# Last layer norm of tile 1's front half built from turned moment rows and two-row products, its input weighted early on GpSimd

## What is computed

```python
def layer_norm(x, g, b):
    mu = jnp.mean(x, axis=-1, keepdims=True)
    var = jnp.mean(jnp.square(x - mu), axis=-1, keepdims=True)
    return (x - mu) * lax.rsqrt(var + LN_EPS) * g + b

hdn = jnp.square(jax.nn.relu(jnp.einsum('bsd,df->bsf', x, w_ff1[l])))
ff_out = jnp.einsum('bsf,fd->bsd', hdn, w_ff2[l])
x = layer_norm(DEEPNORM_ALPHA * x + ff_out, ln2_g[l], ln2_b[l])
```

## Time and profile before

| | |
|---|---|
| device time, median of 3 runs | 1088.48 us (1087.71 to 1088.55) |
| the profiled execution: its own time | 1088.89 us |
| the profiled execution: its span | 1087.1 us, granted TensorE clock 1.000 |
| busy, share of the span: PE, PEld | 1081.4 us (99%), 918.4 us (84%) |
| busy, share of the span: DVE, ACT, POOL | 822.6 us (76%), 578.2 us (53%), 24.5 us (2%) |
| transfers | 213.84 MB, mean 197 GB/s |

### The profile page before, as it was taken

One profiled execution on the slowest core, in us unless ns is written; L12 is line 12 of the kernel. 1 busy time (PEld: TensorE's weight loads), 2 busy tenths in 40 slices (PEclk: granted clock), 3 DMA queues, 4 the chain that ended last, 5 costly groups with the idle time before them and its releaser, 6 DMA issues.

```text
span 1087.1 us, 13951 instructions
## 1 busy us (share of the span) xinstructions
PE 1081.4 (99%) x5586; PEld 918.4 (84%) x5586; DVE 822.6 (76%) x923; ACT 578.2 (53%) x756; POOL 24.5 (2%) x43
## 2 busy tenths in 40 slices
PE   9999999999999999999999999999999999999998
PEld 7888888888888888888888888888888888888886
DVE  6587758666666685667699999766776678889998
ACT  6487757665544524445465456444454455545461
POOL 1000101010000000000000000000000000000000
PEclk9999999999999999999999999999999999999999
DMA  9857665557545835665656566566656655655862
GB/s 300 263 177 224 185 191 156 175 177 247 176 155 168 285 108 156 192 193 176 218 189 231 169 220 232 167 188 191 191 174 204 219 177 198 228 195 190 282 222 78
DMA packets 108048, 213.84 MB, mean 197 GB/s; under 512 B 6784, under 2 KB 38016, under 8 KB 107472
## 3 DMA queue, kind: packets, MB, share of 16 engines
q1 hardware_dynamic: 107216, 209.61, 60.1%
q0 software_dynamic: 624, 3.21, 1.0%
q10 hardware_dynamic: 144, 0.13, 0.0%
HBM read 210.83 MB, written 2.10 MB: 196 GB/s over the span
## 4 chain that ended last, share of the span: by engine, by line
PE 98%; DVE 1%; DMA 1%; issue 0%; SPq 0%; ACT 0%; DVEq 0%
PE low_ps L802 11%; PE low_ps L639 10%; PE high_ps L802 9%; PE high_ps L824 7%; PE high_ps L823 7%; PE high_ps L822 7%; PE low_ps L531 6%; PE low_ps L527 6%; PE low_ps L529 6%; PE low_ps L808 5%; PE high_ps L808 5%; PE low_ps L644 5%; PE low_ps L823 3%; PE low_ps L824 3%; PE low_ps L822 3%; PE high_ps L576 1%
## 5 line engine op out<-in xcount | busy, mean ns | idle before, releaser
L1333 DVE TENSOR_TENSOR w_lo<-w_raw,w_hi 128x1024 fp32r<-128x1024 f32 x175 | 213.1, 1222 | 133.6 <-ACT w_hi L993 132.2
L993 ACT ACTIVATE w_hi<-w_raw 128x1024 fp32r<-128x1024 f32 x175 | 185.1, 1059 | 188.5 <-PE low_ps L531 69.5
L802 PE MATMUL low_ps<-x1T,w_hi 128*128 128x512 f32 x512 | 177.3, 393 | 0.0
L802 PE MATMUL high_ps<-x1T,w_hi 128*128 128x512 f32 x448 | 155.1, 393 | 0.0
L639 PE MATMUL low_ps<-xT,w_hi 128*128 128x512 f32 x448 | 144.2, 398 | 0.0
L808 PE MATMUL low_ps<-x1T,w_lo 128*128 128x256 f32 x512 | 139.3, 278 | 0.0
L1663 DVE TENSOR_TENSOR w_lo<-w_raw,w_hi 128x1024 fp32r<-128x1024 f32 x72 | 87.0, 1222 | 59.7 <-ACT w_hi L1194 59.7
L1218 ACT ACTIVATE sum_hi<-sum_raw 128x1024 fp32r<-128x1024 f32 x60 | 63.6, 1063 | 124.7 <-DVE sum_raw L1685 112.8
L808 PE MATMUL high_ps<-x1T,w_lo 128*128 128x256 f32 x448 | 122.1, 278 | 0.0
L1194 ACT ACTIVATE w_hi<-w_raw 128x1024 fp32r<-128x1024 f32 x72 | 76.1, 1060 | 86.4 <-PE low_ps L802 43.4
L802 PEld LDWEIGHTS low_ps<-x1T,w_hi 128*128 128x128 f32 x512 | 94.9, 187 | 20.1
(11 more groups left out here) (214 smaller groups left out, 1915.4 us busy)
## 6 DMA issues: line engine op xcount, KB each, us to landing
w_raw<-in_w_ff SPq DMA_DIRECT2D x208, 512.0 KB, 4.3
w_raw<-in_w_in SPq DMA_DIRECT2D x93, 512.0 KB, 4.3
more_raw<-in_w_ff SPq DMA_DIRECT2D x42, 512.0 KB, 5.2
w_raw<-in_w_out SPq DMA_DIRECT2D x32, 512.0 KB, 3.7
x_raw<-in_x_turned SPq DMA_DIRECT2D x8, 256.0 KB, 6.4
y<-in_x SPq DMA_DIRECT2D x8, 256.0 KB, 4.6
side_raw<-in_w_ff SPq DMA_DIRECT2D x4, 512.0 KB, 6.7
w_raw<-in_w_in SPq DMA_DIRECT2D x6, 256.0 KB, 5.8
```

Source lines behind the costliest of these rows:

```text
L802: return pe.matmul(banks[:, b, :], w_hi[:, slot, cols], x1T[:, t, :, :].rearrange("p h t -> p (h t)"), start=(t == 0 and not lows_open), s ...
L993: act.activation(w_hi[:, slot, :], w_raw[:, slot, :], ACT.Copy).then_inc(w_rounded, units)
L1333: dve.tensor_tensor(w_lo[:, slot, :], w_raw[:, slot, :], w_hi[:, slot, :].bitcast(F32), ALU.subtract).then_inc(w_split, units)
```

## The change

Tile 1's front half (pieces 3 to 6) is no longer centred by VectorE. The norm is written as (y*g - mean*g + std*b) / std:

- GpSimd multiplies tile 1's front half by g in place, once g and b are loaded and the fourth of the front half's statistics is taken (`y2_stats` 4); then it raises the semaphore `weighted`. Its powers for 1/std stand behind that in its list.
- TensorE puts identity times the weighted y into PSUM for the four pieces. When tile 1's moments are there, it turns the two columns [mean, std] of `mean_std` into two rows by a product with the identity; ScalarE copies these with the signs -1 and +1 into `moment_rows`; TensorE adds the product of these two rows with the two rows [g, b] (`gb_rows`).
- ScalarE takes std with a square root (`last_std`), ahead of tile 1's epsilon instruction; a first square root on a constant stands ahead of the tail. ScalarE copies pieces 3 to 6 out with 1/std as the scale.
- SP loads the two rows of `gb_rows` (4 KB each) behind each broadcast load of g and b.
- Piece 2 is finished by VectorE, last, and stored last by SP; the products and the diagonal for it go. VectorE's order behind tile 1's moments is: centre 7, centre 8, finish 7, finish 8, finish piece 2.
- The stores' order becomes 0, 1, 3, 7, 4, 8, 5, 2 (6 still by ScalarE).
- At the start VectorE fills two more small vectors (`eps_one`, `row_signs`).

The diff without the declarations of tiles and semaphores and without the reshaped helper of the first norm (`first_scale` and `inverse_std`, which issue the same instructions for that norm as `norm_scale(0)` did):

```diff
-COPIED = [2] + SCALED
-STORE_ORDER = [0, 1, 2, 7, 3, 4, 5, 8]
+FIRST_HALF = slice(0, HALF)
+BY_VECTOR = [0, 1, 7, 8, 2]
+STORE_ORDER = [0, 1, 3, 7, 4, 8, 5, 2]
...
+                    sp.dma_start(gb_rows[n:n + 1, :], v[:, FIRST_HALF]).then_inc(rows_loaded, 16)
...
-            if i in COPIED:
-                sp.wait_ge(y2_copied, COPIED.index(i) + 1)
+            if i in SCALED:
+                sp.wait_ge(y2_copied, SCALED.index(i) + 1)
             else:
-                sp.wait_ge(y2_ready, i + 1 - len([n for n in COPIED if n < i]))
+                sp.wait_ge(y2_ready, BY_VECTOR.index(i) + 1)
...
-        pe.wait_ge(tail_summed, 2)
-        pe.wait_ge(gb2_loaded, 32)
-        pe.matmul(high_ps[:, 1, :], ident_t[:, :], ln2_gb[:, 1, LAST_PIECES[2][1]], start=True, stop=False)
-        pe.wait_ge(diag_ready, 1)
-        pe.wait_ge(centred, len(PIECES) + 3)
-        pe.matmul(high_ps[:, 1, :], diag[0][:, :], y1[:, 0, LAST_PIECES[2][1]], start=False,
-                  stop=True).then_inc(y2_scaled, 1)
         pe.wait_ge(low_drained, 4)
+        pe.wait_ge(weighted, 1)
         for i in SCALED:
-            pe.matmul(scaled_ps(i), ident_t[:, :], ln2_gb[:, 1, LAST_PIECES[i][1]], start=True,
-                      stop=False)
-        pe.wait_ge(diag_ready, TT)
-        for n, i in enumerate(SCALED):
-            tt, cols = LAST_PIECES[i]
-            pe.wait_ge(centred, len(PIECES) + (6 if i > 4 else 4))
-            pe.matmul(scaled_ps(i), diag[1][:, :], y1[:, tt, cols], start=False,
+            pe.matmul(scaled_ps(i), ident_t[:, :], y1[:, 1, LAST_PIECES[i][1]], start=True, stop=False)
+        pe.wait_ge(tail_summed, 3)
+        pe.wait_ge(moments, 2 * TT)
+        pe.wait_ge(mean_std_ready, 1)
+        pe.matmul(high_ps[0:2, 2, 0:P], mean_std, ident_t[:, :], start=True, stop=True).then_inc(
+            moments_turned, 1)
+        pe.wait_ge(rows_loaded, 32)
+        pe.wait_ge(rows_ready, 1)
+        for i in SCALED:
+            pe.matmul(scaled_ps(i), moment_rows[0:2, :], gb_rows[0:2, LAST_PIECES[i][1]], start=False,
                       stop=True).then_inc(y2_scaled, 1)
...
-        for tt in range(TT):
-            act.wait_ge(moments, TT + tt + 1)
-            act.activation(var_eps[:, tt:tt + 1], mean_var[:, 2 * tt + 1:2 * tt + 2], ACT.Copy,
-                           bias=EPS).then_inc(var_ready, 1)
-            if tt == 1:
-                act.wait_ge(y2_scaled, 1)
-                act.activation(y1[:, 0, LAST_PIECES[2][1]], high_ps[:, 1, :], ACT.Copy).then_inc(
-                    y2_copied, 1)
-            act.wait_ge(std_ready, TT + tt + 1)
-            act.activation(diag[tt][:, :], ident_t[:, :], ACT.Copy, scale=inv_std[:, tt:tt + 1]).then_inc(
-                diag_ready, 1)
+        act.wait_ge(powers_ready, 5)
+        act.activation(last_std, eps_one, ACT.Sqrt)
+        act.wait_ge(moments, TT + 1)
+        act.activation(var_eps[:, 0:1], mean_var[:, 1:2], ACT.Copy, bias=EPS).then_inc(var_ready, 1)
+        act.wait_ge(moments, TT + 2)
+        act.activation(last_std, mean_var[:, 3:4], ACT.Sqrt, bias=eps_one).then_inc(mean_std_ready, 1)
+        act.activation(var_eps[:, 1:2], mean_var[:, 3:4], ACT.Copy, bias=EPS).then_inc(var_ready, 1)
+        act.wait_ge(moments_turned, 1)
+        act.activation(moment_rows[0:2, :], high_ps[0:2, 2, 0:P], ACT.Copy, scale=row_signs[0:2, :]).then_inc(
+            rows_ready, 1)
+        act.wait_ge(std_ready, 2 * TT)
         for n, i in enumerate(SCALED):
             tt, cols = LAST_PIECES[i]
-            act.wait_ge(y2_scaled, n + 2)
-            act.activation(y1[:, tt, cols], low_ps[:, n, 0:cols.stop - cols.start],
-                           ACT.Copy).then_inc(y2_copied, 1)
+            act.wait_ge(y2_scaled, n + 1)
+            act.activation(y1[:, tt, cols], low_ps[:, n, 0:cols.stop - cols.start], ACT.Copy,
+                           scale=inv_std[:, 1:2]).then_inc(y2_copied, 1)
         for i in BY_SCALAR:
             tt, cols = LAST_PIECES[i]
-            act.wait_ge(y2_copied, SCALED.index(i) + 2)
+            act.wait_ge(y2_copied, SCALED.index(i) + 1)
             act.dma_start(out_d[:, tt, cols], y1[:, tt, cols]).then_inc(stored, 16)
...
+        dve.memset(eps_one, EPS).then_inc(powers_ready, 1)
+        dve.memset(row_signs, 1.0).then_inc(powers_ready, 1)
+        dve.wait_ge(powers_ready, 4)
+        dve.memset(row_signs[0:1, :], -1.0).then_inc(powers_ready, 1)
...
-        def finish_piece(i, centred_before):
-            finish_norm(1, count + centred_before, 1, LAST_PIECES[i][1], y1, ln2_gb, y2_ready)
-
-        centre(1, 1, slice(0, 512), y1, ln2_gb)
         centre(1, 1, LAST_PIECES[7][1], y1, ln2_gb)
-        finish_piece(7, 5)
-        centre(1, 1, slice(512, 1024), y1, ln2_gb)
         centre(1, 1, LAST_PIECES[8][1], y1, ln2_gb)
-        finish_piece(8, 7)
+        finish_norm(1, count + 4, 1, LAST_PIECES[7][1], y1, ln2_gb, y2_ready)
+        finish_norm(1, count + 5, 1, LAST_PIECES[8][1], y1, ln2_gb, y2_ready)
+        finish_norm(1, count + 3, 0, front[2], y1, ln2_gb, y2_ready)
...
+        pool.wait_ge(gb2_loaded, 32)
+        pool.wait_ge(y2_stats, 4)
+        pool.tensor_tensor(y1[:, 1, FIRST_HALF], y1[:, 1, FIRST_HALF], ln2_gb[:, 0, FIRST_HALF],
+                           ALU.mult).then_inc(weighted, 1)
+        inverse_std(1, 0)
+        inverse_std(1, 1)
```

More of the change, by code:

```diff
@@ L175, in hybrid_layer @@
     mid = at("mid", [P, 2 * TT, NC], F32, 48 * KB)
-    diag = [at(f"diag{tt}", [P, P], F32, 48 * KB + 512 * tt) for tt in range(TT)]
+    moment_rows = at("moment_rows", [P, P], F32, 48 * KB)
     X0 = 56 * KB
@@ L221, in hybrid_layer @@
     last_raw = at("last_raw", [P, 4 * NC], F32, H0 + 24 * KB)
+    gb_rows = at("gb_rows", [P, HALF], F32, X0 + 28 * KB)
     own_hi = [at("own_hi0", [P, 3 * NC], F32R, H0 + 77 * KB), at("own_hi1", [P, 3 * NC], F32R, X0)]
@@ L244, in hybrid_layer @@
     eps_sum = part(42, 2)
+    last_std, eps_one, row_signs = part(40, 1), part(44, 1), part(45, 1)
+    mean_std = small[:, 34:41:6]
     stats = part(48, TT * CHUNKS * 6 + 6)
@@ L313, in hybrid_layer @@
     y2_stats, y2_ready, stored = sem("y2_stats"), sem("y2_ready"), sem("stored")
-    diag_ready, y2_scaled, y2_copied = sem("diag_ready"), sem("y2_scaled"), sem("y2_copied")
+    rows_loaded, mean_std_ready, moments_turned = sem("rows_loaded"), sem("mean_std_ready"), sem("moments_turned")
+    rows_ready, y2_scaled, y2_copied = sem("rows_ready"), sem("y2_scaled"), sem("y2_copied")
+    weighted = sem("weighted")
     x_d = x.rearrange("b (t p) d -> p (b t) d", p=P)
@@ L1919, in rms_scale, with inverse_std, first_scale @@
             pool.tensor_tensor(o_scale, root, inv_sums[h % 3][:, 0:4:2], ALU.mult).then_inc(scale_ready, 1)
[L1921 to L1931, removed]
+        def inverse_std(norm, tt):
+            n = TT * norm + tt + 1
+            pool.wait_ge(var_ready, n)
+            pool.tensor_tensor(inv_std[:, tt:tt + 1], var_eps[:, tt:tt + 1],
+                               minus_half[:, tt:tt + 1], ALU.pow).then_inc(std_ready, 1)
+        def first_scale(tt):
+            pool.wait_ge(moments, tt + 1)
+            pool.tensor_scalar(var_eps[:, tt:tt + 1], mean_var[:, 2 * tt + 1:2 * tt + 2], EPS,
+                               None, ALU.add).then_inc(var_ready, 1)
+            inverse_std(0, tt)
         pool.wait_ge(w_used, SLOTS + 1)
@@ L1947, in gpsimd_program @@
                 "p l d -> p (l d)")).then_inc(gb1_loaded, 16)
-        norm_scale(0)
-        norm_scale(1)
+        for tt in range(TT):
+            first_scale(tt)
+        pool.wait_ge(gb2_loaded, 32)
[4 more added lines that the diff above has]
+        inverse_std(1, 1)
     with nc.Block() as block:
```

## The result

| | before | after |
|---|---|---|
| device time, median | 1088.31 us (1087.71 to 1089.05, 15 runs) | 1090.48 us (1089.60 to 1091.81, 15 runs) |
| ratio after / before, 95% interval | | 1.0020 (1.0013 to 1.0027) |
| the profiled execution: its own time, span | 1088.89, 1087.1 us | 1090.55, 1088.7 us |
| granted clock, mean of the span | 1.000 | 0.997 |

The change makes the kernel 2.17 us slower, where 1.6 was forecast (1090.1, range 1088.3 to 1091.5). The profiled execution of before was itself 0.58 above the median of its 15 runs. The two executions also differ ahead of the change: the sum at L1700 (L1692 before) begins at 1049.80 in after and 1050.33 in before.

The account below looks back on a forecast made before the run. The prediction took VectorE's adds, statistics and norm of the last two tiles to bound the end. VectorE held up (+1.2) and stores (+0.4) summed to +1.6 us, 1090.1 on the median, range 1088.3 to 1091.5.

Parts of the forecast that it names:

- the hold: At about 1050 us VectorE's next two-SBUF-operand instruction waits 2.2 us for GpSimd; +1.2 us at the end.
- GpSimd's multiply: Weighting tile 1's front half at about 1049 us: length 2.2 us, between 1.21 and 4.0, costing +1.2 through VectorE.
- the gap: VectorE's only idle time from 1048 us, 0.97 us before 1068.65, waiting for TensorE; expected to absorb that much lateness.
- Its sign of being wrong: In the trace after, GpSimd's multiply at about 1049 us taking under 1.5 or over 2.75 us would refute the forecast.
- No exclusion: Rival, 20%: VectorE runs on while GpSimd multiplies at about 1050 us; only the stores' +0.4 remains, 1088.9.
- The stores: At the kernel's end, tile 0's third piece stored last: between +0.1 and +0.7 us, taken as +0.4.
- until about 3.9 us past the first of these issues: Expected sign at the end: data keeps moving this long after SP's first store issue behind tile 1's moments.
- TensorE "off the path": Behind tile 1's moments: four identity products replace bias and diagonal products, take 1.89 us, done by 1079.9, delaying nothing.
- compute ends 0.55 earlier: Behind tile 1's moments, the new chain's last eviction ends at 1083.6 instead of 1084.17.
- What costs nothing: Ahead of the tail: table load, two one-row loads (about 0.4 us each, 2.5 slack) and three small fills are covered.
- the rival of the tables: Rival, 5%: the copy between the two square roots reloads tables, two loads of 1.28 on the chain, +2.6; 1091.5 without exclusion.
- The long instruction: Rival, 13%: GpSimd's multiply at 1050 us takes up to 4.0 us, each microsecond over 0.97 reaching the end; +3.4, 1091.9.

Follow-up runs that it names:

- e7: The kernel before with only SP's order of stores changed, piece 2 stored last of all; 1089.05 us, ratio 1.0007 to before.
- e2: The changed kernel plus two TensorE products that nobody reads, one in each idle time around the turning of the moments; 1090.14 us, ratio 1.0017 to before.
- e1: The changed kernel with GpSimd's multiply 18 us later, beside VectorE's tail adds and statistics; 1089.26 us, ratio 1.0010 to before.
- e6: The kernel before plus two GpSimd multiplies of 1024 columns, one behind the other, into a spare tile; 1091.28 us, ratio 1.0028 to before.
- e3: The kernel before plus GpSimd's multiply of 1024 columns alone, at the change's place, into a spare tile; 1089.22 us, ratio 1.0010 to before.

## Why the prediction was right in the whole, and where its steps were not

The sum of the parts, each by the distance that only it moves: run-up +1.02 (the hold), tail +0.74 (piece 2 last, e7) and +0.27 (the clock, after against e2), together 2.03; 2.17 was measured. By the medians, with their wide intervals, it is 0.99 + 0.85 + 0.26 = 2.10 (the clock's part as after's distance to before, 2.17, less e2's, 1.91). That the forecast of +1.6 came this near is in part luck: it had too much for the hold, too little for the stores and nothing for the clock, and the first error ran against the other two, by 0.18 against 0.61.

- **GpSimd's multiply: right, in mechanism and size.** Forecast 2.2 us of hold, less 0.97 for the gap, so +1.2; measured 2.09 and +1.02, with the 0.12 of slack in the splits, which the forecast missed. The place was right to within an instruction: the sum behind the 128x1024 one. The length, which the forecast took as the middle between 1.21 and 4.0, is 2.40 where GpSimd ran free (e1) and 2.26 here. Its sign of being wrong, a multiply of over 2.75, is met by the recorded 3.25 as it stands, but not by the work: about 1.0 of the record is waiting. The estimate of 2.25, half of what the Trainium skill's GPSIMD Engine Reference, section 3.1, gives for 2048 columns, agrees with these rows. The rule of the Trainium skill's SBUF — State Buffer, "Who interferes with whom", of which before showed only GpSimd waiting for VectorE, is now shown by rows in the other direction too, and e1 shows its limit: an add with one operand in PSUM and statistics with one input were not held, as the section states as well. "No exclusion" is out: its 1088.9 needed a run-up of 29.04.
- **The stores: the term of the sum that was mis-sized.** The step had two models, the last issue (+0.1) and the flow of 1.31 MB at 327 GB/s (+0.7), and I took the middle, 0.4. The flow's figure was right: e7 measured +0.74 in the tail. The issues' figure was too small even for the issues, whose last one ended 0.48 later in e7 and, relative to the aggregate's end, 0.88 later in after (1085.94) than in before. The earlier trace rows alone did not decide it: before flows at a DMA share of 0.93 there, but at 0.75 in its last two microseconds. A middle between two limits is wrong here in principle: the later of two limits decides. (The sign "until about 3.9 us past the first of these issues" also does not follow from the prediction's own sum, by which data moves from an issue at 1082.25 until 1087.0, 4.75; in after it moved until about 1087.7 from an issue at 1083.16, some 4.5.)
- **TensorE "off the path": the step that failed.** It priced the removed products by their time alone, 1.7 us that nothing waits for. What they did beside was keep TensorE at work while it waited for the moments; without them, and with the moments made 1.02 late by the hold, its granted clock fell to the lower level and the four two-row products took 3.58 instead of 1.89. So "compute ends 0.55 earlier" was wrong for the change (it ended 5.48 after the aggregate, 1.0 later than before's 4.5), though right for the same chain in e1 (3.86). The two edits had been priced apart, and their meeting was not: in e1, without the hold, the idle time was 0.23 and the clock stayed.
- **Why that failure cost so little.** In after the last data moves without a pause, at a share of 0.99. So about the later start of the flow counts alone, 0.27 by the tail. From the forecast's +1.6 to the measured +2.17 it goes by 0.18 too much for the hold, 0.34 too little for the stores, 0.27 missing for the clock, and 0.14 that the parts leave over.
- **What costs nothing: right.** The added table load, of 1.28, stands at 1062.06, where ScalarE is idle, and none stands behind 1079; the rival of the tables is out. In the trace of after no wait shows for the two one-row loads.
- **The long instruction: right in its mechanism.** e6 made it by doubling, and it came to +3.08. Its condition, 2.75 us of hold, was not met.

What stays open: how the last tenths divide. e2 and after differ by 0.27 in the tail and 0.34 in the medians, within what the medians can tell from nothing; that the clock fell and made the products long is shown by e2's rows, what it is worth at the end is carried by single executions. And the price of piece 2's place is measured, while its reading as bytes and not as issues is argued.

## What to carry to other kernels

Before putting work onto an idle engine, look at what the neighbour runs beside it: the same GpSimd multiply cost 1 us next to VectorE sums of two SBUF operands and held none of VectorE's instructions next to adds out of PSUM. Where the final stores move without a pause, time the end by when the first store starts and how many bytes are left, not by when the last result is ready. And count products that nothing waits for as a cost only after asking what TensorE does in their place: idle time just ahead of the last chain was paid in clock.

## What the runs showed of the hardware

- The recorded time of an instruction contains its wait for the other engine: GpSimd's multiply reads 3.25 beside VectorE's sum and 2.40 without, VectorE's sum of 512 columns 2.78 and 0.69. The same wait thus stands nowhere as idle time.
- The granted clock fell at the end of the kernel after an idle time of 1.25 us, a product pair of 0.38 and another idle time of 0.54. With idle times of 0.23 and 0.54 around the same products (e1) it did not fall, and neither did it behind a single idle time of 0.74 (e3, ahead of 1082.41) or 0.95 (e6, ahead of 1083.98).
